# Triangular inverses of two linear mixers: odd token tiles' products cross to the other half of the array and back

## The reference

```
a_mat = beta[..., :, None] * jnp.einsum('nhcid,nhcjd->nhcij', k, k) * d_strict
rhs = jnp.concatenate([beta[..., None] * v, (beta * gam)[..., None] * k], axis=-1)
sol = lax.linalg.triangular_solve(a_mat, rhs, left_side=True, lower=True, unit_diagonal=True)
```

## Time and profile before

| | us |
|---|---|
| median of 3 runs | 1995.14 |
| the runs | 2004.53, 1994.45, 1995.14 |
| span of the profiled execution, first to last instruction | 2001.2 |
| PE busy in the span | 1764.2 (88%) |
| DVE busy in the span | 857.6 (43%) |
| ACT busy in the span | 592.7 (30%) |

### The profile page before, as it was taken

How to read it: one execution, slowest core, us unless ns; L and a number is a source line. 1 busy time by engine, 2 the same in 40 slices (tenths; PEclk the granted TensorE clock), 3 DMA queues, 4 the chain that set the end, 5 groups by cost and what they waited for, 6 DMA issues and landing times.

```text
span 2001.2 us, 44027 instructions
## 1 busy us (share of the span) xinstructions
PE 1764.2 (88%) x17970; PEld 1033.3 (52%) x17970; DVE 857.6 (43%) x1514; ACT 592.7 (30%) x1018; POOL 243.5 (12%) x270
## 2 busy tenths in 40 slices
PE   5998895977778877898999899999989998899996
PEld 2444543544444444445865784354447856853452
DVE  1567524111111111367666753151457747642331
ACT  3314521000000000334324424252253325424442
POOL 0002211111111111006112100001002103000001
PEclk8998996999999999998999999999999999999998
DMA  9758025999999999521000003110211000012101
GB/s 358 259 197 291 1 69 220 370 423 424 423 424 424 425 424 413 216 74 33 3 3 2 3 20 109 42 43 32 80 43 35 3 2 2 4 65 104 42 1 42
DMA packets 75098, 307.75 MB, mean 154 GB/s; under 512 B 10908, under 2 KB 22300, under 8 KB 57888
## 3 DMA queue, kind: packets, MB, share of 16 engines
q1 hardware_dynamic: 63280, 291.98, 37.2%
q0 software_dynamic: 5360, 9.33, 1.3%
q10 hardware_dynamic: 6272, 3.81, 0.6%
HBM read 301.01 MB, written 16.52 MB: 159 GB/s over the span
## 4 chain that ended last, share of the span: by engine, by line
PE 73%; DVE 13%; another core or an unknown queue 6%; ACT 4%; issue 3%; DMA 1%; DVEq 0%; ACTq 0%; POOL 0%; POOLq 0%
PE bank L2253 12%; PE bank L496 12%; PE bank L2269 6%; PE bank L1027 6%; PE bank L525 5%; PE bank L532 4%; PE bank L2091 3%; PE bank L2175 3%; PE bank L998 2%; DVE arena L1596 2%; ACT arena L1039 1%; PE bank L512 1%; PE bank L2115 1%; PE bank L2103 1%
## 5 line engine op out<-in xcount | busy, mean ns | idle before, releaser
L496 PE MATMUL bank<-hT,arena 128*128 128x512 f32 (+1 forms) x640 | 287.7, 605 | 3.6 <-ACTq L1040 2.4
L2253 PE MATMUL bank<-arena 128*64 128x256 f32 x1792 | 216.3, 399 | 66.9 <-remote 66.9
L525 PE MATMUL bank<-arena 64*64 64x64 f32 x6656 | 215.5, 220 | 22.7 <-DVE arena L1726 7.2
L525 PEld LDWEIGHTS bank<-arena 64*64 64x64 f32 x6656 | 203.8, 136 | 37.0 <-DVE arena L1726 10.1
L2253 PEld LDWEIGHTS bank<-arena 128*64 128x64 f32 x1792 | 135.6, 143 | 158.0 <-issue 107.8
L496 PEld LDWEIGHTS bank<-hT,arena 128*128 128x128 f32 (+1 forms) x640 | 122.9, 194 | 161.2 <-issue 156.6
L2859 DVE COPY arena<-bank 128x256 f32<-128x256 f32 x32 | 13.6, 425 | 329.6 <-PE bank L2261 329.6
L2269 PE MATMUL bank<-arena 128*64 128x512 f32 x448 | 104.0, 606 | 16.4 <-remote 16.4
L1027 PE MATMUL bank<-arena 128*128 128x512 f32 x256 | 110.4, 593 | 0.0
L1039 ACT ACTIVATE arena<-bank 128x512 f32<-128x512 f32 (+2 forms) x124 | 73.2, 590 | 118.9 <-PE bank L496 79.2
L532 PE MATMUL bank<-hT,arena 128*128 128x512 f32 x224 | 105.0, 607 | 1.7 <-remote 1.7
(11 more groups left out here) (448 smaller groups left out, 2677.1 us busy)
## 6 DMA issues: line engine op xcount, KB each, us to landing
arena<-w_gate SPq DMA_DIRECT2D x28, 2048.0 KB, 30.6
arena<-w_up SPq DMA_DIRECT2D x28, 2048.0 KB, 21.0
arena<-w_down SPq DMA_DIRECT2D x28, 2048.0 KB, 26.2
arena<-w_ada SPq DMA_DIRECT2D x12, 2048.0 KB, 19.7
arena<-w_in SPq DMA_DIRECT2D x10, 2048.0 KB, 11.7
arena<-w_out SPq DMA_DIRECT2D x6, 2048.0 KB, 7.6
arena<-w_in SPq DMA_DIRECT2D x6, 1536.0 KB, 6.9
hT<-w_up SPq DMA_DIRECT2D x4, 2048.0 KB, 20.9
```

The lines of the kernel that those rows point to most:

```text
L496: m = pe.matmul(bank[b][0:w, :], slot2(n)[:, k, c:c + w], hT[:, k, :], start=(k == 0), stop=(k == KD - 1))
L525: m = pe.matmul(o[half(f), s, t], lhs[half(f), s, t], rhs[half(f), s, t], start=True, stop=True)
L2253: mm = pe.matmul(bank[b][c * CAP:(c + 1) * CAP, 0:FE // 2], XT[j][:, k % 4, k // 4, :], e_slot(e_at(e, i), KD)[:, k, c * (FE // 2):(c + 1) ...
```

## The change

Token tiles are split by parity, t = 2a + j. `crossing` takes the place of `product` for V: even tiles (j=0) as before, odd tiles (j=1) read `half(f)` and write `half(1-f)`. `returning` makes Y^T V: odd tiles read V on the half where it now lies, and bring the result back to `half(f)`. For that the odd tiles' Y has to lie on the other half as well: DVE transposes it straight to there, into the new tile `Y_odd` (which uses the memory of `rs`). So in each of the levels 1 to 4 one transpose of 128x512 becomes one of 128x256 (even tiles) and two of 64x256 (odd tiles, across halves); at level 4 one of 128x256 is added, since level 5 and what follows need the odd tiles of Y on their own half too. At the start of a pass, two copies of 64x256 for each direction fill `Y_odd`. PE's second product of a level waits for `y_odd_full` as well. Both products of direction d now lie in banks 2d and 2d+1, split by parity, V in columns 0 to 255 and Y^T V in 256 to 511; at level 1 the V product waits for both banks to be free, where before only the second product waited for bank 2+d. The last product of a pass goes to bank 2d, `decay_rows` of the next pass to banks 1 and 3, and the value transpose of ht=1 to bank 0.

```diff
+        Y_odd = [rs[:, 256 * d:256 * d + 256].rearrange("p (a n) -> p a n", n=CG) for d in range(2)]
+        def results(d, part):
+            return banks[:, 2 * d:2 * d + 2, 256 * part:256 * part + 256].rearrange("p j (a n) -> p j a n", n=CG)
+        def by_parity(ap):
+            return ap.rearrange("p (a j n) -> p a j n", j=2, n=CG)
...
+            four = [(j, f) for j in range(2) for f in range(2)]
+            def crossing(o, lhs, rhs):
+                lhs, rhs = by_parity(lhs), by_parity(rhs)
+                for a in range(TT):
+                    for j, f in four:
+                        m = pe.matmul(o[half(f ^ j), j, a], lhs[half(f), j, a], rhs[half(f), j, a], start=True, stop=True)
+                return m
+            def returning(o, Y, Y_odd, V, last):
+                Y, V = by_parity(Y), by_parity(V)
+                for a in range(TT):
+                    for j, f in four:
+                        y = Y_odd[half(1 - f), a] if j else Y[half(f), 0, a]
+                        v = V[half(f ^ j), j, a]
+                        m = pe.matmul(o[half(f), j, a], v if last else y, y if last else v, start=True, stop=True)
+                return m
...
                     for l in range(1, LEVELS):
                         for d in range(2):
+                            if l == 1:
+                                for j in range(2):
+                                    pe.wait_ge(bank_free[2 * d + j], 1)
                             t_full[d].wait()
-                            product(d, g_Bn[d], g_T[d]).then_inc(sem(f"g_v_done{d}"), 1)
+                            crossing(results(d, 0), g_Bn[d], g_T[d]).then_inc(sem(f"g_v_done{d}"), 1)
                         for d in range(2):
                             v_full[d].wait()
-                            y_full[d].wait()
-                            if l == 1:
-                                pe.wait_ge(bank_free[2 + d], 1)
-                            if l < LEVELS - 1:
-                                product(2 + d, g_Y[d], g_V[d]).then_inc(sem(f"g_t_done{d}"), 1)
-                            else:
-                                product(2 + d, g_V[d], g_Y[d]).then_inc(sem(f"g_t_done{d}"), 1)
+                            y_full[d].wait(2 if l == LEVELS - 1 else 1)
+                            y_odd[d].wait(2)
+                            returning(results(d, 1), g_Y[d], Y_odd[d], g_V[d],
+                                      l == LEVELS - 1).then_inc(sem(f"g_t_done{d}"), 1)
...
-                            act.activation(g_V[d], bank[d], ACT.Copy).then_inc(sem(f"g_v_full{d}"), 1)
+                            act.activation(by_parity(g_V[d]), results(d, 0), ACT.Copy).then_inc(sem(f"g_v_full{d}"), 1)
...
+            def turned_blocks(d, l, Y, Tm):
+                Y2, T2 = by_parity(Y), by_parity(Tm)
+                dve.transpose(Y2[:, 0], T2[:, 0]).then_inc(sem(f"g_y_full{d}"), 1)
+                for f in range(2):
+                    dve.transpose(Y_odd[d][half(1 - f)], T2[half(f), 1]).then_inc(sem(f"y_odd_full{d}"), 1)
+                if l == LEVELS - 2:
+                    dve.transpose(Y2[:, 1], T2[:, 1]).then_inc(sem(f"g_y_full{d}"), 1)
...
                         dve.transpose(g_T[d], g_Y[d]).then_inc(sem(f"g_t_full{d}"), 1)
+                        for f in range(2):
+                            dve.tensor_copy(Y_odd[d][half(1 - f)], by_parity(g_Y[d])[half(f), 1]).then_inc(sem(f"y_odd_full{d}"), 1)
...
-                                dve.copy_predicated(blocks(g_T[d]), merged(d, l, False), blocks(bank[2 + d])).then_inc(sem(f"g_t_full{d}"), 1)
+                                dve.copy_predicated(by_parity(g_T[d]), merged_parity(d, l, False), results(d, 1)).then_inc(sem(f"g_t_full{d}"), 1)
                                 n_t[d] += 1
                                 dve.wait_ge(sem(f"g_t_full{d}"), n_t[d])
-                                dve.transpose(g_Y[d], g_T[d]).then_inc(sem(f"g_y_full{d}"), 1)
+                                turned_blocks(d, l, g_Y[d], g_T[d])
```

More of the change, by code:

```diff
@@ L403, in merged, with merged_parity @@
             return over_blocks(c2[:, a:a + CG].bitcast(U32))
+        def merged_parity(d, l, upper):
+            a = C2["up" if upper == (d == 0) else "low"][0] + l * CG
+            return c2[:, a:a + CG].bitcast(U32).rearrange("p (j a n) -> p j a n", j=1, a=1).to_broadcast([P, 2, TT, CG])
         def chunk_at(d, n):
@@ L535, in shifted, with decay_rows @@
                     m.then_inc(for_act[b], 1)
-            def decay_rows(ht, b):
+            def decay_rows(ht, at):
                 for d in range(2):
@@ L542, in decay_rows @@
                         for t, f in pairs_in:
-                            m = pe.matmul(pieces(bank[b + d])[half(f), s, t], g_g[half(f), t, c + s:c + s + 1].to_broadcast([CG, CG]),
+                            m = pe.matmul(pieces(bank[at[d]])[half(f), s, t], g_g[half(f), t, c + s:c + s + 1].to_broadcast([CG, CG]),
                                           const2("cum" + name)[half(f), half(f)], start=True, stop=True)
@@ L565, in gdn_chunks @@
                                                    ("g_t_full", "g_y_full", "g_v_full", "g_uw_free")]
-                rk_full = [Count(pe, sem(f"g_rk_full{d}")) for d in range(2)]
+                rk_full, y_odd = [[Count(pe, sem(f"{n}{d}")) for d in range(2)] for n in ("g_rk_full", "y_odd_full")]
                 kk_free = Count(pe, sem("g_kk_free"))
@@ L576, in gdn_chunks @@
                     if ht > 0:
-                        decay_rows(ht, 0)
+                        decay_rows(ht, (1, 3))
                         for d in range(2):
@@ L624, in gdn_chunks @@
                 kk_free.wait()
-                for n in t_full + y_full + v_full + rk_full + [kk_free, v_ch]:
+                for n in t_full + y_full + y_odd + v_full + rk_full + [kk_free, v_ch]:
                     n.clear()
@@ L694, in rwkv_chunks @@
                 in_full, bt_full, k_free = [Count(pe, sem(n)) for n in ("r_in_full", "r_bt_full", "r_k_free")]
+                y_odd = [Count(pe, sem(f"y_odd_full{d}")) for d in range(2)]
                 for b in range(4, 8):
@@ L732, in rwkv_chunks @@
                             t_full[d].wait()
-                            product(d, r_Bn[d], r_bt[:, ct, d]).then_inc(sem(f"g_v_done{d}"), 1)
+                            crossing(results(d, 0), r_Bn[d], r_bt[:, ct, d]).then_inc(sem(f"g_v_done{d}"), 1)
                         for d in range(2):
-                            Y, V = r_kmt[:, ct, d], r_kr[:, ct, d, 0]
                             v_full[d].wait()
-                            y_full[d].wait()
-                            if l < LEVELS - 1:
-                                product(2 + d, Y, V).then_inc(sem(f"g_t_done{d}"), 1)
-                            else:
-                                product(2 + d, V, Y).then_inc(sem(f"g_t_done{d}"), 1)
+                            y_full[d].wait(2 if l == LEVELS - 1 else 1)
+                            y_odd[d].wait(2)
+                            returning(results(d, 1), r_kmt[:, ct, d], Y_odd[d], r_kr[:, ct, d, 0],
+                                      l == LEVELS - 1).then_inc(sem(f"g_t_done{d}"), 1)
                     if ct == 1:
@@ L747, in rwkv_chunks @@
                         y_full[d].wait()
-                        product(2 + d, r_kmt[:, ct, d], r_BT[d]).then_inc(sem(f"g_u_done{d}"), 1)
+                        product(2 * d, r_kmt[:, ct, d], r_BT[d]).then_inc(sem(f"g_u_done{d}"), 1)
                     for d in range(2):
@@ L756, in rwkv_chunks @@
                     m.then_inc(sem("g_w_done"), 1)
-                for n in t_full + y_full + v_full + [in_full, bt_full, k_free]:
+                for n in t_full + y_full + y_odd + v_full + [in_full, bt_full, k_free]:
                     n.clear()
@@ L858, in pe_second @@
                             take(pe, bank_free[2 + d])
-                        decay_rows(0, 2)
+                        decay_rows(0, (2, 3))
                         for d in range(2):
@@ L1182, in act_second @@
                         u_done[d].wait()
-                        chain.mark(act.activation(g_u0[d][:, :, 2 * ht:2 * ht + 2, :].rearrange("p t s n -> p s t n"), pieces(bank[2 + d]),
+                        chain.mark(act.activation(g_u0[d][:, :, 2 * ht:2 * ht + 2, :].rearrange("p t s n -> p s t n"), pieces(bank[2 * d]),
                                              ACT.Copy))
@@ L1263, in act_second @@
                             v_done[d].wait()
-                            act.activation(r_kr[:, ct, d, 0], bank[d], ACT.Copy).then_inc(sem(f"g_v_full{d}"), 1)
+                            act.activation(by_parity(r_kr[:, ct, d, 0]), results(d, 0), ACT.Copy).then_inc(sem(f"g_v_full{d}"), 1)
                         if ct == 0 and l in (2, 3):
@@ L1268, in act_second @@
                         u_done[d].wait()
```

(6 more changed lines are left out.)

23 lines of the change are left out of this document (12 added, 11 removed).

## The result

The changed kernel takes 2050.9 us (median of 4 runs, 2045.6 to 2052.5) against 1994.8 of the kernel before in the same comparison: 1.027 times as long, 95% interval 1.025 to 1.030. It is slower, as forecast, but by 56 us where 17 were predicted, and it lies above the range of 1992 to 2028. The profiled execution spans 2049.1 us. In the kernel after, the crossing product is L542, the returning one L551; the narrow transposes are L1497 (even tiles), L1499 (odd tiles, two for each half level) and L1501 (the one added at level 4); the merges L1631 and L1763 (level 5: L1636, L1768); the copies at a pass's start L1621 and L1756.

What follows compares the result with a forecast made beforehand. A level was taken as bounded by DVE for its first half and two PE products for its second. Passes losing 21.3 us, less 4.5 gained at their starts, made 16.8 slower than the median of 1995.1: 2012, range 1992 to 2028.

Steps and rivals of the forecast that it cites:

- What the change does to PE: Level products: all four combinations of halves work at once, 32 loads go from 0.98 to 0.55, 0.45 taken as saved.
- The rival at 2029: Level products: four at once is not reached, a product stays at 0.98, time 2029; chance 0.09.
- What it does to DVE: Levels 1 to 4: narrow transposes 0.45 each, starting 0.38 apart; 0.50 more per half level, 4.8 us more per pass.
- The end that it gave for no overlap: Narrow transposes in the levels: upper bound of 0.45 from start to start; with copies of 0.30 it gives 2030.
- The sum by pass: Levels of each pass: 4.8 more DVE work less DVE's idle time; 10.9 lost in first layer, 10.4 in second, 21.3 together.
- The clean level of 3.87: Level with no extra work, as in ct=1: PE's way falls from 4.27 to 3.87, a gain of 0.40.
- The starts of the passes: Pass starts: shorter products and cheaper copies give 4.5 back together, though the first layer's ht=0 loses 0.5.
- After the levels nothing changes: Behind the levels of each pass: no change, since the last products wait for the same merges.
- a rival of 0.10, the falling clock: Products after the levels in ct=0: PE idles more, its clock falls, they double; 6 us more, 2018; chance 0.10.
- the sign of a granted clock near 1.00 in the passes: Profile after the change: TensorE's granted clock was expected near 1.00 in the passes.
- The range: Whole kernel: 1992 to 2028 us; the bounds of the transpose alone give 1989 and, with copies of 0.30, 2030.

Runs made afterwards that it cites:

- e11: e9 with ACT instead of VectorE also making the odd-tile copies at the start of ht=0; 1994.5 us, 0.999 of before.
- e2: The change with all VectorE work kept, but products back to two combinations of halves (computes another product); 2063.8 us, 1.034 of before.
- e10: The change with eight more 64x64 matmuls, output unread, ahead of each crossing product; 2051.1 us, 1.028 of before.
- e9: The change with VectorE's one 128x512 transpose back and ACT copying Y's odd tiles across ahead of its V copy; 1993.8 us, 1.000 of before.
- e3: The change with the two 64-row odd transposes made one of 128 rows that crosses nothing (computes another product); 1997.5 us, 1.001 of before.
- e4: The change with both 64-row odd transposes writing the half they read (computes another product); 2038.7 us, one run.
- e8: The change with TensorE transposing the odd tiles across halves, ACT copying them behind V, VectorE transposing even tiles alone; 2016.8 us, 1.011 of before.

## Why the prediction was wrong, by its own steps

**What the change does to PE: right.** Four combinations at once were reached, with the row of L621 as the measure: 32 loads in 0.56 against 0.55 predicted, two halves writing one bank notwithstanding. The rival at 2029 fell. The Trainium skill spoke for it (TensorEngine Tiling, "Restrictions and Gotchas": no two row tiles in one PSUM bank at once), and for a slower product by its floor of about 25 ns from start to start (TensorE: Matmul & The Clock Gate, "Wait — 56ns, not 53.3ns?"); the 0.56, 17 ns a load, agrees with neither.

**What it does to DVE: the direction right, the size wrong, and this is the step that failed.** "0.45 each" holds to 10 ns; "the next starting after 0.38" does not. The 0.07 of overlap came from a row in which both instructions begin at partition 0, and was given to instructions that begin at 64 or write there. The price stood in the trace of before, in the 64x384 row that the prediction used for its fixed part. L1623 works on one chunk's 64 rows, and L1626 behind it on 128 rows from partition 0. Behind an L1623 on the upper half (1042.59) L1626 starts 0.58 later, behind one on the lower half (1043.57) 0.47:

```profile
1042.59 0.56 DVE L1623 TENSOR_TENSOR arena<-arena,bank 64x384 f32<-64x384 f32 x1 [1.97 <-PE bank L645]
1043.17 0.36 DVE L1626 TENSOR_TENSOR arena<-arena 128x192 f32<-128x192 f32 x1
1043.57 0.55 DVE L1623 TENSOR_TENSOR arena<-arena,bank 64x384 f32<-64x384 f32 x1
1044.04 0.34 DVE L1626 TENSOR_TENSOR arena<-arena 128x192 f32<-128x192 f32 x1
```

In the change it is 0.47 from start to start, so 0.78 for a half level and 1.15 with the added transpose at level 4 (2.55 from merge to merge). The prediction's own pass sum then reads 6 x 0.78 + 2 x 1.15 = 7.0 in place of 4.8. The end that it gave for no overlap was 0.45, a duration; the hand-over costs 0.02 to 0.03 more, so even its bound was too low, at 2030.

**The sum by pass: the rule right.** 7.0 less VectorE's idle time of before gives 6.2, 2.3, 5.1, 7.0 and 1.3 for the first layer; measured 5.6, 2.3, 5.4, 7.2 and 1.9. For both layers that is 43.3 against 45.8 measured, where 0.38 had given 21.3. So 22 of the 39 us that the forecast missed are this one number. The clean level of 3.87 never appeared, since VectorE bounds ct=1 too.

**The starts of the passes: half right.** Predicted 4.5 back, measured 2.7. ht=1, ht=2 and both ct passes gained 0.0 to 0.8 each; ht=0 of the first layer lost 2.6 in place of 0.5. The overlap failed here too: the prediction let a pair of copies occupy 0.46, but the next instruction starts 0.64 after the start of a pair (975.33 to 975.97), and the copies start 0.74 after the transpose ahead of them (974.59) where its successor had started after 0.64 before the change. A pair of copies takes 0.61 in ht=1, but at 928.07 a pair took 2.04, beside two of GpSimd's operations without a gap:

```profile
928.07 2.04 DVE L1621 COPY rs<-arena 64x256 f32<-64x256 f32 x2
...
975.33 0.61 DVE L1621 COPY rs<-arena 64x256 f32<-64x256 f32 x2
...
926.73 1.88 POOL L1419 TENSOR_SCALAR xT<-xT,p 128x512 f32<-128x512 f32 x1
928.69 1.27 POOL L1420 TENSOR_TENSOR xT<-xT,arena 128x512 f32<-128x512 f32 x1
```

GpSimd was idle during the pair in ht=1. That it is GpSimd that stretches them was not tested: e11 took the copies away from there, and the time did not move.

**"After the levels nothing changes": wrong,** by 7.9 us in two layers. The prediction named the main cause in a rival of 0.10, the falling clock, with the right place (products behind the levels), but for ct=0 alone and at 6 us; there the ledger has 2.5 for both layers, and the rest lies behind the passes of ht. With it failed the sign of a granted clock near 1.00 in the passes. It was wrong to hold it against the forecast as an alternative: where VectorE holds a level longer and PE's products get shorter, PE idles in it, so the clock's cost belongs on top of VectorE's, and in ht=0 above all. It is shown for ht=0 of the first layer by e2 and e10 (11.5 again at a clock of 1.00), and for ct=0 by e9, whose stretch takes 12.57 at 0.86 in the first layer and 11.02 at 1.00 in the second (before: 11.30 and 11.01, both at 1.00). Not all of the 7.9 is the clock: behind ht=1 of the first layer e2 takes 0.43 more than before at 1.00, half of the change's 0.87, and that part is open.

**The range** took its upper end from the transposes' and copies' bounds and put nothing on top for the clock. Of the 56.1 us between the medians the ledger holds 51.0 and the two traces show 2.0 more outside the passes; the remaining 3.1 are in no row.

## What to carry to other kernels

Before one wide VectorE instruction is split by partitions, count the instructions that begin at another partition than their predecessor: each loses its overlap. A row of full-height neighbours does not show that price; look for neighbours whose first partition changes. When an engine's work grows inside a loop that TensorE shares, and TensorE's own work there gets shorter, add what TensorE's clock then costs behind the loop; it comes on top. A gain of TensorE that needs its operand moved has to pay for the move: ACT made it partly inside a wait in e9, and the time still came out as before.

## What the runs showed that was not expected

VectorE's hand-over takes 0.33 to 0.37 us for a 256-column transpose if the rows begin where the last ones did, and 0.42 to 0.48 if not, always after the end of the one ahead (e3, e4 and the change). Sixteen matmuls that write one pair of banks from both halves into both halves run at the pace of L621: 0.56 for 32 loads, 17 ns each. At that pace PE can stand still for up to 2.0 us in or ahead of a product at full granted clock (e8: 22 us in all); the waits of 0.3 us or more end 2.3 to 2.9 us after a 16 KiB transfer of its instructions started, which speaks for their supply as the limit.
